# A two-block transformer kernel on one core: the mLSTM part re-cut around g3, ba0 and ba1, o/i/f as 260 + 260 columns, and six held blocks at the end

## The chip, the cores and the metric

The kernel runs on one core of one Trainium2 chip. The metric is the device time of one execution in microseconds, the median of three runs. The profile is that of one further execution.

## What is computed

Two blocks over 256 tokens of width 1024, batch 1. All in float32; a weight product is made as three products of rounded parts (high x high, high x low, low x high).

```
h = modulate(rms_norm(x, g_pre_mix), shift_m, scale_m)
q_a,k_a,v_a, q_m,k_m,v_m, o_m,i_m,f_m, g_a,g_m = split(h @ w_in)
y_a = sliding_window_attention(rope(q_a), rope(k_a), v_a, sinks)
q_m,k_m = split(silu(causal_depthwise_conv([q_m,k_m])))
h_m = mlstm_chunkwise(q_m, k_m, v_m, i_m + b_i, f_m + b_f)      # 4 heads of 128, chunks of 64
    # num = (q k' * w_intra) v + w_inter * q C_prev ; den likewise ; h = num / max(|den|, exp(-m))
y_m = sigmoid(o_m) * head_layer_norm(h_m, mlstm_norm_w)
merged = sigmoid(g_a) * (y_a @ w_branch_attn) + sigmoid(g_m) * (y_m @ w_branch_mlstm)
x = x + gate_m * rms_norm(merged @ w_out)
x = x + gate_f * rms_norm(swiglu(modulate(rms_norm(x))) @ w_ffn_down)
# second block: gMLP and RWKV-7 mixing, then the same kind of feed-forward, and at its very end
x = layer_norm(ALPHA * x + gt2 * f, ln2_g, ln2_b)
```

## The kernel before

Every engine's program is one list written out by hand; semaphores tie the lists together. The weights come as a stream of 512 KB blocks through six slots of `raw` (SyncE issues a block when VectorE has given up the slot, line 450). For each block ScalarE makes the rounded high part `whi` (`split`, line 559) and VectorE the low part `wlo` (`prepare`, line 416), in `HL = 4` slots each; ScalarE may write a slot when TensorE has done the block that was in it (`blocks_done`). Blocks named c0 to c21 belong to the modulation vectors: VectorE sums them into `acc` (lines 433 and 437), and TensorE adds them up over the partitions in `part(d)` with products of one column (line 1914).

The order of items on TensorE is o_if, qm, km, vm, g0, qa, kva, g1, g2, g3, ba0, ba1, bm0, bm1, wo0, wo1, then the feed-forward. `tokens_out` (lines 1958 to 1960) puts tokens on the rows of the result, `features_out` (1983 to 1985) features. The names that matter here:

- o_if has 520 columns: i and f (8) and o (512). The 8 go to banks 4 and 5, the 512 to the item's own pair. ScalarE takes the sigmoid of o into `osig` (line 610).
- `between(i)` runs on TensorE behind g3's blocks 0, 1, 2: states of the mLSTM (`chunk_kv`) and the turned attention scores (`turn_scores`, line 2141), which wait for ScalarE's exponentials (`score_exps`, 693 and 695).
- Behind g3: the attention's products with v for 128 tokens (o0, line 2165), `part(3)`, the same for the other 128 (o1, line 2172), `intra_part(0)` (line 2183: the mLSTM's product within its chunks for tokens 0 to 127), the turns of y_a (line 2204), `inter_part(0)` (2194: the part with the carried states), `intra_part(1)`, `inter_part(1)`.
- VectorE divides y_a by the sums of scores (1317), adds inter to intra (`take_inter`, 1328), makes the low half `yal` of the turned y_a (1352), takes each head's mean and variance (`head_stats`, 1341 to 1346), and multiplies by `osig` (1382) to `ym`. ScalarE copies intra out of its bank (722), copies `yah` (728), takes the root of the variances (734) and scales the eight heads (739).
- `turn_ym` (2217) turns ym on TensorE behind ba1; ScalarE copies `ymh`, VectorE makes `yml` (1388); bm0 and bm1 need both. `by_gate` (1375) multiplies a branch by its gate and frees its banks.
- `down_block(t, m, c)` (2245 to 2247) adds block t of the last weights for row half m and column half c into bank 4 + 2m + c. The first 22 - 4 blocks run block by block; the last four, held in the four slots, run row by row: (m, c) = (0,0), (0,1), (1,0), (1,1), each over all four blocks, so that a quarter of the result is done early. VectorE then weighs a quarter and adds it (`residual`, lines 1422, 1819, 1508) and finishes a row half in `last_rows` (1848 to 1853).

Of the kernel before, what the change touches and what calls it, by code (L numbers as in the profile page):

```python
# [8 lines left out]
D = 1024  # L9
P = 128  # L10
MT = S // P
# [9 lines left out]
HL = 4  # L21
# [126 lines left out]
def build(nc, A, out):  # L148
# [5 lines left out]
    with ctx:  # L154
# [24 lines left out]
        hl = rounded("hl", ARENA + 2048, [KT, S])  # L179
        raw = sb("raw", [P, RAW, SLOT])  # L180
# [206 lines left out]

        def part_place(d):
            return {0: (0, 0), 1: (1, 0), 2: (2, 0), 3: (4, 0), 4: (6, 0), 5: (4, 0), 6: (4, 6), 7: (4, 7),
                    8: (2, 8), 9: (2, 9), 10: (6, 0), 11: (4, 0)}[d]  # L390
# [16 lines left out]
        def prepare_on(eng, me, name, part=slice(None)):  # L407

            for b in sorted(at_block[name] + at_block.get(with_piece(name), []))[part]:
# [4 lines left out]
                if g is not None:  # L414
                    eng.wait_ge(sem("hi_ready"), g + 1)
                    eng.tensor_tensor(wlo[:, g % HL, 0:nk * width], raw[:, b % RAW, 0:nk * width],  # L416
                                      whi[:, g % HL, 0:nk * width].bitcast(fp), ALU.subtract)\
# [98 lines left out]
        def _(act):  # L516
# [34 lines left out]
            def split(name, part=slice(None)):  # L551

                for b in at_block[name][part]:
                    _, _, nk, width, _, count, g = order[b]
                    act.wait_ge(sem(f"raw{b % RAW}_in"), count)
                    if g >= HL:

                        act.wait_ge(sem("blocks_done"), g - HL + 1)
                    act.activation(whi[:, g % HL, 0:nk * width], raw[:, b % RAW, 0:nk * width], ACT.Copy)\  # L559
# [50 lines left out]
            act.activation(osig[:, 0, :], b0[:, :], ACT.Sigmoid).then_inc(sem("osig_ready"), 1)  # L610
            freed("o_if", act.activation(osig[:, 1, :], b1[:, :], ACT.Sigmoid))
# [97 lines left out]

            take_turned(0, 2)  # L710
            split("ba0", slice(0, 1))
            take_turned(2, 4)
            split("ba0", slice(1, 2))
# [5 lines left out]
            for m in range(MT):  # L719
                for h2 in range(2):  # L720
                    act.wait_ge(sem("intra_done"), 2 * m + h2 + 1)
                    act.activation(intra[:, m, 2 * h2:2 * h2 + 2, :],
                                   bank[4 + h2][:, 0:258].rearrange("p (h n) -> p h n", h=2),
                                   ACT.Copy).then_inc(sem("intra_ready"), 1)
                if m == 0:
                    for i in range(MT):
                        act.wait_ge(sem("ya_turned"), i + 1)
                        act.activation(yah[:, :, i * P:(i + 1) * P],
                                       bank[2 + i][:, :].rearrange("p (i n) -> p i n", i=4),
                                       ACT.Copy).then_inc(sem("yah_ready"), 1)  # L730

            split("bm0", slice(0, 1))
            act.wait_ge(sem("hvar_ready"), 1)
            act.activation(st[:, 112:120], st[:, 112:120], ACT.Sqrt).then_inc(sem("hstd_ready"), 1)
            act.wait_ge(sem("hvar_ready"), 2)
            for m in range(MT):
                for h in range(HM):
                    n = 4 * m + h
                    ins = act.activation(intra[:, m, h, 0:128], intra[:, m, h, 0:128], ACT.Identity,
                                         bias=st[:, 144 + n:145 + n], scale=st[:, 112 + n:113 + n])  # L740
                ins.then_inc(sem("hstd_ready"), 1)
            split("bm0", slice(1, 2))
# [239 lines left out]
        def _(dve):  # L982
# [137 lines left out]
            item("o_if")  # L1120
            dve.wait_ge(sem("spreads"), 3 * 16)
            for m in range(MT):
                TT(st[:, 240 + 8 * m:248 + 8 * m], bank[4 + m][:, 0:8], bsm[:, 0:8], ALU.add)\
                    .then_inc(sem("if_ready"), 1)

            dve.wait_ge(sem("osig_ready"), 1)
# [186 lines left out]
            collect_part(3)  # L1313
            prepare("ba1", slice(0, 1))
            for m in range(MT):
                dve.wait_ge(sem("o_done"), m + 1)
                TT(ya[:, m, :].rearrange("p (h c) -> p h c", h=HQ), bank[m][:, :].rearrange("p (h c) -> p h c", h=HQ),
                   bcast(st[:, 32 + 8 * m:40 + 8 * m], 64), ALU.mult)\
                    .then_inc(sem("ya_ready"), 1)
            prepare("ba1", slice(1, 2))  # L1320
# [1291 lines left out]
```

## Time and profile before

| | |
|---|---|
| median of 3 runs | 861.46 us (861.17 to 861.91) |
| the profiled execution | 863.23 us, its span 861.4 us |
| TensorE busy | 809.8 us, 94% |
| VectorE busy | 640.3 us, 74% |
| ScalarE busy | 390.0 us, 45% |
| mean granted clock of TensorE | 0.98 |

Busy times count instructions that run, not waits. Products on TensorE are pipelined: one of 512 columns is shown with about 0.39 us but the next starts 0.23 us later, so starts are to be compared and not durations.

### The profile page before, as it was taken

The numbers are of one execution on the slowest core, as the hardware profiler recorded it, in microseconds if no ns is written. First come the engines' busy times: TensorE is split into PE (matmuls) and PEld (weight loads), VectorE is DVE, ScalarE is ACT, GpSimd is POOL, SyncE is SP. The second block draws the span as 40 slices with busy tenths as digits, with TensorE's granted clock in tenths as the row PEclk, the third lists the DMA queues.
The fourth block names the chain that finished last, engine by engine and source line by source line (L and its number), as shares of the span: only waits on it lengthen the run. The fifth ranks groups of instructions, "written<-read, shape, count | busy, mean of one in ns | idle before, by whom it ended". The sixth has DMA issues, their size and how long they took to land.

```text
span 861.4 us, 16653 instructions
## 1 busy us (share of the span) xinstructions
PE 809.8 (94%) x7026; PEld 739.0 (86%) x7026; DVE 640.3 (74%) x841; ACT 390.0 (45%) x540; POOL 12.6 (1%) x32
## 2 busy tenths in 40 slices
PE   2899999899799999999998999989998999999995
PEld 2798998898678999999887987889977999999883
DVE  5859878858978877867877899887478777455447
ACT  3346843834255444444244884521134544444331
POOL 0100000000000000000001000000000000000000
PEclk9899999979999999999999999999999999999998
DMA  9974656761766978988883634610043669465521
GB/s 364 334 257 157 192 177 213 232 206 56 240 224 234 348 241 279 324 269 305 332 302 98 226 121 134 208 53 4 27 149 122 211 221 346 153 190 176 198 95 49
DMA packets 95832, 173.71 MB, mean 202 GB/s; under 512 B 7575, under 2 KB 55038, under 8 KB 95758
## 3 DMA queue, kind: packets, MB, share of 16 engines
q1 hardware_dynamic: 92784, 165.86, 57.5%
q0 software_dynamic: 1744, 5.84, 2.1%
q8 instruction: 55, 0.90, 0.4%
q10 hardware_dynamic: 1230, 0.95, 0.4%
q14 instruction: 19, 0.16, 0.1%
HBM read 171.58 MB, written 1.05 MB: 200 GB/s over the span
## 4 chain that ended last, share of the span: by engine, by line
PE 74%; DVE 17%; ACT 4%; issue 2%; DMA 2%; DVEq 0%; SPq 0%; ACTq 0%
PE bank L1983 13%; PE bank L1985 12%; PE bank L1984 12%; PE bank L2245 4%; PE bank L2247 4%; PE bank L2246 4%; DVE acc L437 3%; PE bank L2415 3%; PE bank L1958 2%; DVE wlo L416 2%; PE bank L1959 2%; PE bank L1960 2%; PE bank L1914 1%; DMA raw<-in_w_in 1%; DVE arena L437 1%
## 5 line engine op out<-in xcount | busy, mean ns | idle before, releaser
L559 ACT ACTIVATE whi<-raw 128x1024 fp32r<-128x1024 f32 (+2 forms) x218 | 226.8, 1051 | 271.3 <-PE bank L1985 122.6
L416 DVE TENSOR_TENSOR wlo<-raw,whi 128x1024 fp32r<-128x1024 f32 (+2 forms) x218 | 261.9, 1214 | 110.1 <-ACT whi L559 106.8
L1983 PE MATMUL bank<-hh,whi 128*128 128x256 f32 x1016 | 287.0, 282 | 3.2 <-DVE hl L1071 2.9
L1985 PE MATMUL bank<-hh,wlo 128*128 128x256 f32 x1016 | 285.2, 281 | 0.0
L1984 PE MATMUL bank<-hl,whi 128*128 128x256 f32 x1016 | 285.2, 281 | 0.0
L1983 PEld LDWEIGHTS bank<-hh,whi 128*128 128x128 f32 x1016 | 192.3, 189 | 6.1 <-issue 5.6
L1985 PEld LDWEIGHTS bank<-hh,wlo 128*128 128x128 f32 x1016 | 191.6, 189 | 0.0
L1984 PEld LDWEIGHTS bank<-hl,whi 128*128 128x128 f32 x1016 | 191.4, 188 | 0.1
L437 DVE SCALAR_TENSOR_TENSOR acc<-raw,cc,acc 128x1024 f32<-128x1024 f32 x77 | 98.6, 1280 | 7.3 <-DMA raw<-in_w_ada 3.4
L2245 PE MATMUL bank<-whi,ffh 128*128 128x512 f32 x176 | 69.6, 396 | 0.7 <-DVE wlo L416 0.7
L2246 PE MATMUL bank<-wlo,ffh 128*128 128x512 f32 x176 | 69.3, 394 | 0.0
L2247 PE MATMUL bank<-whi,ffl 128*128 128x512 f32 x176 | 69.2, 393 | 0.0
L1958 PE MATMUL bank<-whi,hh 128*128 128x512 f32 (+2 forms) x112 | 41.8, 373 | 0.7 <-DVE wlo L416 0.7
L1959 PE MATMUL bank<-wlo,hh 128*128 128x512 f32 (+2 forms) x112 | 41.3, 369 | 0.0
L1960 PE MATMUL bank<-whi,hl 128*128 128x512 f32 (+2 forms) x112 | 41.2, 368 | 0.0
L2245 PEld LDWEIGHTS bank<-whi,ffh 128*128 128x128 f32 x176 | 33.1, 188 | 9.1 <-DVE wlo L416 1.6
L2247 PEld LDWEIGHTS bank<-whi,ffl 128*128 128x128 f32 x176 | 33.1, 188 | 7.7
L2246 PEld LDWEIGHTS bank<-wlo,ffh 128*128 128x128 f32 x176 | 33.0, 188 | 7.4
L812 ACT ACTIVATE ffh<-arena 128x512 fp32r<-128x512 f32 x22 | 13.9, 632 | 46.8 <-DVEq L1480 46.8
L2415 PE MATMUL bank<-arena 64*64 64x64 f32 x896 | 28.0, 218 | 3.1 <-DVEq L1700 1.8
L2415 PEld LDWEIGHTS bank<-arena 64*64 64x64 f32 x896 | 27.1, 134 | 4.0 <-DVEq L1700 1.9
L1994 PE MATMUL bank<-cst 128*128 128x256 bf16 x220 | 28.7, 293 | 0.0
(430 smaller groups left out, 1027.4 us busy)
## 6 DMA issues: line engine op xcount, KB each, us to landing
raw<-in_w_ada SPq DMA_DIRECT2D x96, 512.0 KB, 5.0
raw<-in_w_in SPq DMA_DIRECT2D x54, 512.0 KB, 4.6
raw<-in_w_ffn_in SPq DMA_DIRECT2D x88, 256.0 KB, 3.7
raw<-in_w_ffn_gate SPq DMA_DIRECT2D x44, 256.0 KB, 4.0
raw<-in_w_ffn_up SPq DMA_DIRECT2D x44, 256.0 KB, 5.1
raw<-in_w_ffn_down SPq DMA_DIRECT2D x22, 512.0 KB, 5.5
raw<-in_w_ffn_out SPq DMA_DIRECT2D x22, 512.0 KB, 3.2
raw<-in_w_out SPq DMA_DIRECT2D x16, 512.0 KB, 5.1
```

The lines of the kernel that those rows point to most:

```text
L416: eng.tensor_tensor(wlo[:, g % HL, 0:nk * width], raw[:, b % RAW, 0:nk * width], whi[:, g % HL, 0:nk * width].bitcast(fp), ALU.subtract)\
L437: eng.scalar_tensor_tensor(to, x, by, to, ALU.mult, ALU.add)\
L559: act.activation(whi[:, g % HL, 0:nk * width], raw[:, b % RAW, 0:nk * width], ACT.Copy)\
L1958: mm(dsts[m], xh[:, kk_, t], wh[:, k, c], start=first, stop=False)
L1959: mm(dsts[m], xh[:, kk_, t], wl[:, k, c], start=False, stop=False)
L1983: mm(o, wh[:, k, c], xh[:, kk_, :], start=first, stop=False)
L1984: mm(o, wh[:, k, c], xl[:, kk_, :], start=False, stop=False)
L1985: last = mm(o, wl[:, k, c], xh[:, kk_, :], start=False, stop=end)
L2245: mm(o, ffh[:, t, x], wh[:, 0, cs], start=(t == 0), stop=False)
L2246: mm(o, ffh[:, t, x], wl[:, 0, cs], start=False, stop=False)
L2247: return mm(o, ffl[:, t, x], wh[:, 0, cs], start=False, stop=(t == FT - 1))
L2415: last = mm(bank[4 + 2 * (n % 2) + h][r, L * (q % 8):L * (q % 8) + L], lhsT[r, q, :], rhs[r, q, :], start=True, stop=True)
```

## The change

1. o_if is cut at column 260 instead of 8: columns 260 to 519 go to banks 4 and 5, columns 0 to 259 to the item's own pair. Each of 48 pairs of products (8 and 512 columns) becomes a pair of 260 and 260. ScalarE takes two sigmoids of 252 columns and two of 260. i and f are read from the end of banks 4 and 5.
2. `intra_part(0)` moves between g3's blocks, into banks 6 and 7; behind g3 stand o0, `inter_part(0)`, `part(3)`, o1, the first turn of y_a, `intra_part(1)`, the second turn, `inter_part(1)`.
3. VectorE and ScalarE normalise y_m by halves of 128 tokens: `head_stats(0)`, `head_var(0)` and `head_shift(0)` move ahead of ba0, and ScalarE's scaling of half 0 with them.
4. `turn_ym` moves from behind ba1 to behind its first block.
5. In the second feed-forward six blocks are held: the last two have places of their own, `whl` and `wll`, in the memory of `hh` and `hl`, free when gf10 is done. `last_rows(0)` moves ahead of `residual(1, 0)`.

```diff
+        whl = rounded("whl", ARENA, [2, D])
+        wll = rounded("wll", ARENA + 2048, [2, D])
...
+        HELD = HL + 2
+
+        def weight_place(g):
+            j = g - (split_n - 2)
+            return (whl[:, j], wll[:, j]) if j >= 0 else (whi[:, g % HL], wlo[:, g % HL])
...
-                    if g >= HL:
+                    if g >= split_n - 2:
+
+                        act.wait_ge(sem("blocks_done"), place[f"gf{FT // 2 - 1}"][2])
+                    elif g >= HL:
...
-            act.activation(osig[:, 0, :], b0[:, :], ACT.Sigmoid).then_inc(sem("osig_ready"), 1)
-            freed("o_if", act.activation(osig[:, 1, :], b1[:, :], ACT.Sigmoid))
+
+            for m in range(MT):
+                act.activation(osig[:, m, 260:512], bank[4 + m][:, 0:252], ACT.Sigmoid)
+            act.activation(osig[:, 0, 0:260], b0[:, 0:260], ACT.Sigmoid).then_inc(sem("osig_ready"), 1)
+            freed("o_if", act.activation(osig[:, 1, 0:260], b1[:, 0:260], ACT.Sigmoid))
...
             take_turned(2, 4)
+            take_intra(0, 6)
             split("ba0", slice(1, 2))
...
+            normalise(0)
+            for i in range(MT):
+                act.wait_ge(sem("ya_turned"), i + 1)
+                act.activation(yah[:, :, i * P:(i + 1) * P], bank[2 + i][:, :].rearrange("p (i n) -> p i n", i=4),
+                               ACT.Copy).then_inc(sem("yah_ready"), 1)
+                if i == 0:
+                    take_intra(1, 4)
+            split("bm0", slice(0, 1))
+            normalise(1)
             split("bm0", slice(1, 2))
...
             take_inter(0)
+            collect_part(3)
+            prepare("ba1", slice(0, 1))
+            divided(0)
+            head_stats(0)
+            head_var(0)
+            divided(1)
+            head_shift(0)
+            prepare("ba1", slice(1, 2))
+            gains(1, v1T[:, v1["g_pre_ffn"][0]:v1["g_pre_ffn"][1]])
...
             take_inter(1)
...
+            head_stats(1)
+            head_var(1)
+            weigh_y(0)
+            head_shift(1)
             prepare("bm0", slice(0, 1))
...
+            weigh_y(1)
             by_gate("ba0", 0)
...
-            tokens_out("o_if", 512, modulated, extra=512, half_ready=0)
+            tokens_out("o_if", 260, modulated, extra=260, half_ready=0)
...
+                if i == 1:
+
+                    pe.wait_ge(sem("state_ready"), 4)
+                    intra_part(0, 6)
+                    turn_scores(2, 4)
+                if i == 2:
+                    turn_scores(4, 6)
+                    pe.wait_ge(sem("intra_ready"), 2)
+                    chunk_kv(2, 6)
...
+            turn_ya(0)
+            pe.wait_ge(sem("piece_used"), 4)
+            intra_part(1, 4)
+            turn_ya(1)
             inter_part(1)
...
-            features_out("ba1", four, (yah, yal))
-            turn_ym()
+            features_out("ba1", four, (yah, yal), inside={0: turn_ym})
...
-                for t in range(FT - HL):
+                held = HELD if n else HL
+                for t in range(FT - held):
...
             ln_var(0)
+            dve.wait_ge(sem("ln_var"), 5)
+            last_rows(0)
             dve.wait_ge(sem("rows_done"), 9)
             residual(1, 0, bank[6])
-            dve.wait_ge(sem("ln_var"), 5)
-            last_rows(0)
```

TensorE's list from g3's last block to ba0, before:

```order
L1985 MATMUL bank<-hh,wlo 128x256
L2165 MATMUL bank<-arena 128x64 x8
L1914 MATMUL bank<-cst,acc 128x1 x8
L2172 MATMUL bank<-arena 128x64 x16
L2183 MATMUL bank<-arena,bc 128x129 x4
L2204 MATMUL bank<-cst,arena 128x128 x8
L2194 MATMUL bank<-arena 64x129 x8
L2183 MATMUL bank<-arena,bc 128x129 x4
L2194 MATMUL bank<-arena 64x129 x8
L1983 MATMUL bank<-yah,whi 128x256
```

The same place of the changed kernel (2224 and 2234 are o0 and o1, 1952 the piece, 2185 intra, 2196 inter, 2240 the turns of y_a):

```order
L2023 MATMUL bank<-hh,wlo 128x256
L2224 MATMUL bank<-arena 128x64 x8
L2196 MATMUL bank<-arena 64x129 x8
L1952 MATMUL bank<-cst,acc 128x1 x8
L2234 MATMUL bank<-arena 128x64 x16
L2240 MATMUL bank<-cst,arena 128x128 x4
L2185 MATMUL bank<-arena,bc 128x129 x4
L2240 MATMUL bank<-cst,arena 128x128 x4
L2196 MATMUL bank<-arena 64x129 x8
L2021 MATMUL bank<-yah,whi 128x256
```

One intra part has left this stretch, the first inter part stands ahead of the piece, and the two turns are parted by the other intra part.

VectorE's list behind the end of `head_stats(1)` up to yml, before (416 low halves of blocks, 1375 gate, 1382 weighing of y, 1388 yml):

```order
L1359 TENSOR_TENSOR st<-st 128x8
L1360 SCALAR_TENSOR_TENSOR st<-st 128x8
L1361 RECIPROCAL st<-st 128x8
L416 TENSOR_TENSOR wlo<-raw,whi 128x1024
L1365 SCALAR_TENSOR_TENSOR st<-st 128x8
L1375 TENSOR_TENSOR arena<-bank,arena 128x512 x2
L1382 TENSOR_TENSOR arena<-arena 128x512 x2
L1388 TENSOR_TENSOR yml<-bank,ymh 128x4x128 x2
```

The same place of the changed kernel (427 low halves, 1417 gate, 1385 weighing, 1425 yml):

```order
L1372 TENSOR_TENSOR st<-st 128x4
L1373 SCALAR_TENSOR_TENSOR st<-st 128x4
L1374 RECIPROCAL st<-st 128x4
L1385 TENSOR_TENSOR arena<-arena 128x512
L1379 SCALAR_TENSOR_TENSOR st<-st 128x4
L427 TENSOR_TENSOR wlo<-raw,whi 128x1024
L1385 TENSOR_TENSOR arena<-arena 128x512
L1417 TENSOR_TENSOR arena<-bank,arena 128x512 x2
L1425 TENSOR_TENSOR yml<-bank,ymh 128x4x128 x2
```

The variance is that of one half here; y's first half is weighed before the block of bm0 and its second before the gate of ba0.

## Rows read from the trace of the kernel before

**Rows 1.** The page: TensorE's busy time, and the chain that ended last by engine
```profile
PE 809.8 (94%) x7026; PEld 739.0 (86%) x7026; DVE 640.3 (74%) x841; ACT 390.0 (45%) x540; POOL 12.6 (1%) x32
PE 74%; DVE 17%; ACT 4%; issue 2%; DMA 2%; DVEq 0%; SPq 0%; ACTq 0%
```
**Rows 2.** Waits of TensorE: total us, times, longest us
```profile
PE bank L1958 <- DVE wlo L416: 5.6, 4, 3.8
```
**Rows 3.** Timeline, TensorE at o_if and qm's start: start, us, instruction, [idle before]
```profile
35.29 0.25 PE L1958 MATMUL bank<-whi,hh 128*128 128x8 f32 x1
...
36.63 0.48 PE L1958 MATMUL bank<-whi,hh 128*128 128x512 f32 x1
...
51.87 0.28 PE L1983 MATMUL bank<-hh,whi 128*128 128x256 f32 x1
51.99 0.27 PE L1984 MATMUL bank<-hl,whi 128*128 128x256 f32 x1
```
**Rows 4.** Timeline, TensorE from g3's second block to ba0
```profile
169.07 1.09 PE L2141 MATMUL bank<-cst,xn 128*128 128x128 f32 x8 [2.40 <-ACT st L695]
...
177.83 1.89 PE L2165 MATMUL bank<-arena 128*128 128x64 f32 x16
180.19 2.14 PE L1914 MATMUL bank<-cst,acc 128*128 128x1 f32 x16 [0.47 <-DVE acc L437]
182.20 7.07 PE L2172 MATMUL bank<-arena 128*128 128x64 f32 x32
189.06 2.04 PE L2183 MATMUL bank<-arena,bc 128*128 128x129 f32 x8
190.88 1.60 PE L2204 MATMUL bank<-cst,arena 128*128 128x128 f32 x8
192.42 1.11 PE L2194 MATMUL bank<-arena 128*64 128x129 f32 x16
193.46 1.16 PE L2183 MATMUL bank<-arena,bc 128*128 128x129 f32 x8
```
**Rows 5.** One window: length, busy per engine, granted clock, DMA share, GB/s
```profile
181.80:192.00 10.20, 10.20 (x50) 10.20 (x50) 4.06 (x7) 0.79 (x3) 0.00 (x0) 0.50 0.37 126
```
**Rows 6.** Timeline around ba0 and bm0, of VectorE, ScalarE and TensorE
```profile
195.63 1.38 DVE L1328 SCALAR_TENSOR_TENSOR arena<-bank,st,arena 128x129 f32<-128x129 f32 x4
...
203.23 1.23 DVE L416 TENSOR_TENSOR wlo<-raw,whi 128x1024 fp32r<-128x1024 f32 x1
...
209.28 1.33 DVE L1388 TENSOR_TENSOR yml<-bank,ymh 128x512 fp32r<-128x512 f32 x2 [0.73 <-ACT ymh L745]
...
204.62 3.19 ACT L739 ACTIVATE arena<-arena,st 128x128 f32<-128x128 f32 x8 [1.24 <-DVEq L1366]
...
210.66 0.39 PE L1983 MATMUL bank<-ymh,whi 128*128 128x256 f32 x1 [1.41 <-DVE yml L1388]
...
226.15 0.75 PE L1958 MATMUL bank<-whi,mgh 128*128 128x512 f32 x1 [3.84 <-DVE wlo L416]
```
**Rows 7.** Timeline of the end: ScalarE, TensorE, VectorE
```profile
834.13 1.06 ACT L559 ACTIVATE whi<-raw 128x1024 fp32r<-128x1024 f32 x1 [1.73 <-PE bank L2247]
...
842.04 0.50 PE L2245 MATMUL bank<-whi,ffh 128*128 128x512 f32 x1 [0.35 <-DVE wlo L416]
...
848.62 0.69 DVE L1422 TENSOR_TENSOR xn<-bank,gg 128x512 f32<-128x512 f32 x1 [0.32 <-PE bank L2247]
...
853.65 0.68 DVE L1422 TENSOR_TENSOR xn<-bank,gg 128x512 f32<-128x512 f32 x1
```
**Rows 8.** Timeline, VectorE and ScalarE, low and high parts of blocks, 37 to 47 us
```profile
37.22 3.54 DVE L416 TENSOR_TENSOR wlo<-raw,whi 128x1040 fp32r<-128x1040 f32 x3
46.34 2.36 DVE L416 TENSOR_TENSOR wlo<-raw,whi 128x1024 fp32r<-128x1024 f32 x2 [5.58 <-ACT whi L559]
...
45.25 2.01 ACT L559 ACTIVATE whi<-raw 128x1024 fp32r<-128x1024 f32 x2 [6.89 <-issue]
```
**Rows 9.** Timeline, VectorE: start of the convolution, and of the mLSTM columns
```profile
66.70 0.41 DVE L1144 TENSOR_SCALAR arena<-arena,v1T 128x256 f32<-128x256 f32 x1 [0.88 <-ACT arena L620]
...
111.46 0.19 DVE L1221 COPY st<-bank 128x32 f32<-128x32 f32 x1 [3.28 <-PE bank L2048]
```

More of the change, by code:

```diff
@@ L708, in take_turned, with take_intra @@
                                    ACT.Copy).then_inc(sem("pT_ready"), 1)
+            def take_intra(m, at):
+                for h2 in range(2):
+                    act.wait_ge(sem("intra_done"), 2 * m + h2 + 1)
+                    act.activation(intra[:, m, 2 * h2:2 * h2 + 2, :],
+                                   bank[at + h2][:, 0:258].rearrange("p (h n) -> p h n", h=2),
+                                   ACT.Copy).then_inc(sem("intra_ready"), 1)
             take_turned(0, 2)
@@ L717, in _, with normalise @@
             split("ba1", slice(1, 2))
[L719 to L736, printed above, removed]
+            def normalise(m):
+                q = slice(112 + 4 * m, 116 + 4 * m)
+                act.wait_ge(sem("hvar_ready"), 2 * m + 1)
+                act.activation(st[:, q], st[:, q], ACT.Sqrt).then_inc(sem("hstd_ready"), 1)
+                act.wait_ge(sem("hvar_ready"), 2 * m + 2)
                 for h in range(HM):
@@ L1312, in _ @@
                 step(dve.reciprocal(st[:, 32 + 8 * m:40 + 8 * m], st[:, 32 + 8 * m:40 + 8 * m]))
[L1313 to L1320, printed above, removed]
-            gains(1, v1T[:, v1["g_pre_ffn"][0]:v1["g_pre_ffn"][1]])
             def take_inter(m):
@@ L1887, in weights @@
                 pe.wait_ge(sem(f"{who}_blocks"), count)
[L1888 removed]
+                hi, lo = (w[:, 0:nk * width].rearrange("p (k n) -> p k n", k=nk) for w in weight_place(g))
+                return i, nk, hi, lo
             def part(d):
@@ L2196, in inter_part, with between, turn_ya @@
                     last.then_inc(sem("inter_done"), 1)
-            intra_part(0)
-            for m in range(MT):
+            def between(i):
+                if i == 0:
+                    pe.wait_ge(sem("sw_ready"), 2)
+                    chunk_kv(1, 6)
+                    turn_scores(0, 2)
+                if i == 1:
[6 more added lines that the diff above has]
+                    chunk_kv(2, 6)
+            pe.wait_ge(sem("piece_used"), 3)
+            features_out("g3", four, modulated, inside={i: (lambda i=i: between(i)) for i in range(3)})
+            pe.wait_ge(sem("pT_ready"), 6)
+            pe.wait_ge(sem("va_ready"), 1)
+            for h in range(HQ):
+                g = h // 4
+                last = mm(bank[0][:, 64 * h:64 * h + 64], pT[:, h, :], va[:, 0, 64 * g:64 * g + 64],
+                          start=True, stop=True)
+            last.then_inc(sem("o_done"), 1)
+            pe.wait_ge(sem("state_ready"), 6)
+            inter_part(0)
+            part(3)
+            for h in range(HQ):
+                g = h // 4
+                for kb in range(2):
+                    last = mm(bank[1][:, 64 * h:64 * h + 64], pT[:, 8 + 2 * h + kb, :], va[:, kb, 64 * g:64 * g + 64],
+                              start=(kb == 0), stop=(kb == 1))
+            last.then_inc(sem("o_done"), 1)
+            def turn_ya(m):
                 pe.wait_ge(sem("ya_ready"), m + 1)
-                if m == 0:
-                    pe.wait_ge(sem(f"pair{place['g3'][0] % 2}_free"), place["g3"][0] // 2 + 1)
                 for i in range(4):
@@ L2260, in feed_forward @@
                     for c in range(2):
-                        for t in range(FT - HL, FT):
+                        for t in range(FT - held, FT):
                             last = down_block(t, m, c)
```

90 lines of the change are left out of this document (32 added, 58 removed).

## The prediction

> **What bounds the kernel now.** I read the page first: the shares of busy time and the chain that ended last. TensorE is busy for 94% of the span and carries 74% of the chain, VectorE 17% [rows 1]. So a change can gain in three ways only: fewer cycles on TensorE, filled gaps on TensorE, or a shorter end after its last product. The view of waits says that the gaps are few: the longest waits for VectorE are 5.6 us in four pieces, at the start of wo0 [rows 2]. I then read the timeline of each engine at the four places that the diff touches. Every time below is on the scale of the profile before; an event that comes earlier only because everything before it is earlier keeps its number.
>
> At o_if (35.29 to 51.87 us) TensorE has no gap [rows 3]. Each of its four blocks has 12 products of 8 columns and 12 of 512. The first 12 take 36.63 - 35.29 = 1.34 us, 0.112 us from start to start, though they move 8 columns; the whole block takes 16.58 / 4 = 4.15 us, so the wide ones have 2.81 / 12 = 0.234 us. In the item behind it the step between products of 256 columns is 51.99 - 51.87 = 0.12 us. Small products are nearly as dear as products of 256 columns.
>
> Between g3's end and ba0 (177.83 to 195.8 us) TensorE is nominally busy, but from 181.8 to 192 us at half clock, 0.50 granted, the level of 1.2 GHz [rows 4, 5]. Ahead of the fall stand a gap of 0.47 us and 16 products of one column. The second 129-wide intra part takes 1.16 us at full clock, the first 2.04 at half. There is also a gap of 2.40 us before the turn of scores at 169.07, ended by ScalarE's exponentials.
>
> After ba1, TensorE turns ym and waits for yml: bm0 starts at 210.66 us [rows 6]. VectorE then does a chain of fixed work (ba1's and bm0's gates, four pieces, the low half of merged, wo0's first block) and wo0 starts at 226.15, after an idle stretch of 3.84 us. From bm0's start on, this stretch is VectorE's.
>
> At the end TensorE's last but one row block goes to VectorE at 848.62, but `last_rows(0)` stands ahead of the last residual, which starts at 853.65 [rows 7].
>
> **The parts, worked out.**
>
> *o, i, f as 260 + 260.* Removed: 48 products of 8 columns and 48 of 512, 16.58 us [rows 3]. Added: 96 of 260 columns. No row has 260; the bounds are 0.112 us (8 columns) and 0.234 us (512), the nearest row 0.12 us (256). With 0.12: 96 x 0.12 = 11.5 us, 5.0 us less. Not all of it arrives. Block 1's low half is made at 37.22 + 1.2 = 38.4, and block 0 now ends at 35.29 + 2.88 = 38.17: 0.3 us of waiting. Three more blocks end at 47.1. ScalarE's queue splits qm's first block only at 45.25, behind its own issues of small transfers (its 6.89 us of idleness are put down to issue), and VectorE's part starts at 46.34 and takes some 1.2 us [rows 8]. So qm starts at 47.6 and not at 51.87: **4.3 us** earlier. ScalarE's two sigmoids become four of half the width; it waits for TensorE there, and the splits for km have until 59 us, so I cost them at nothing (without that cover about 0.6 us).
>
> Does it stay? VectorE starts the convolution 0.88 us after its last work, when ScalarE has copied qm, and later waits 3.28 us for TensorE's columns at 111.46 [rows 9]. Both starts hang on TensorE's progress, so they move with it, and all that is released by them too. The transfers from 52 us on are issued when VectorE gives up a slot of `raw`, so they move as well. I keep 4.3.
>
> The Trainium skill, "TensorE: Matmul & The Clock Gate", section on 56 against 53.3 ns, gives start to start at full clock as the columns by 2.4 GHz plus about 2.5 ns. By that rule an 8-column product would cost 5.8 ns and o_if the same before and after, so this part would bring nothing and the sum would be 857.1. The trace disagrees for narrow products: 112 ns.
>
> *The first intra part between g3's blocks.* It goes into the 2.40 us gap before the turn at 169.07, where its four heads (1.16 us at full clock) are free: states and banks are there by 166 us. ScalarE takes it over behind `take_turned(2, 4)`, some 0.8 us, which delays ba0's second split and with it VectorE by some 0.35 us. Behind g3 the order is now o0, inter 0, piece 3, o1, turn, intra 1, turn, inter 1. At full clock inter 0 adds 1.1 us and covers the gap of 0.47. Piece 3's one-column products remain, so I expect the clock to fall as before, near the end of piece 3, and o1 to take its 7 us again: o1 ends at 180.8 + 2.05 + 7.0 = 189.85 (189.06 before). What follows is shorter by one intra part (2.04) and inter 0 (1.1): first turn to 190.75, intra 1 to 192.6, second turn to 193.2. But ba0 needs yal, and the halves of y now compete with it. VectorE must have `divided(1)` done (190.7) before the shift, ScalarE then scales four heads (half of its 3.19 us for eight [rows 6]) to 192.6, copies yah 0, takes intra 1 (0.8), copies yah 1 to 194.5; yal follows at 195.2. So ba0 starts at 195.2, not 195.8: **0.6 us**. If the clock stays up, this same chain on ScalarE and VectorE holds ba0 at about 194.5.
>
> *y by halves, ym's turn inside ba1.* From ba0's start: its two blocks take 5.7 us (as every pair of 24 x 0.12), to 200.9; ba1's first block to 203.8. Inter 1 of VectorE takes 1.3 us; statistics and variance of both halves took from 196.9 to 203.2, so one half takes about 3.5, to 200.1. Half 0 of y is weighed by 200.8; ScalarE scales half 1 from 201.1 to 202.7; its weighing ends at 203.4. The turn in ba1 at 203.8 thus has 0.4 us to spare. It takes about 1.0 us, ba1 ends at 207.65, and yml is ready at 206.4 (before 210.6), 1.2 us to spare. bm0 starts at 207.65 instead of 210.66: **3.0 us**, the 0.6 among them. The VectorE chain from bm0's end to wo0 is the same instructions, so wo0 moves by 3.0 too, to 223.1, with the same idle stretch before it. Behind it VectorE feeds wo0 block by block; all shifts.
>
> *Six held blocks, last rows reordered.* The row-wise part now has 6 x 3 products of 0.2315 us, 4.17 us for a quarter where it had 2.78. It starts 5.56 us earlier, at 833.85. ScalarE may split block 19 at 834.13 as before [rows 7]; 20 and 21 follow at some 1 us each (two take 2.01), VectorE at 1.14 to 1.18 us each (three take 3.54) [rows 8], so block 21 is ready at 838.7, and TensorE, which wants it at 837.3, waits some 1.2 us in all, against 0.35 now. TensorE ends 0.9 us later. VectorE, however, has residual (0,1) at 844, `last_rows(0)` to 849.3 and residual (1,0) to 851.4, and is free when the last quarter arrives at 851.97 + 0.33 = 852.3, not 853.65: **1.35 us** gained. Without the waits it would be 2.2.
>
> **Sum.** 4.3 + 3.0 + 1.35 = 8.65 us. The profiled execution: 863.23 us, span 861.4; it becomes 854.6 and 852.8. It stands 1.8 us over the median; from the median 861.46 the forecast is **852.8 us**.
>
> **Rivals.**
> - *The clock falls elsewhere* (0.14). Half clock comes in stretches, and every one falls at another instruction once the work moves. If the one before bm0 or a later one is missed, TensorE gains 1.5 to 3 us where it is the bound: 850.5. Speaks for it: the cost of a stretch on real work is half its length. Against: behind g3 and at wo0 other engines hold the time.
> - *The second half waits for VectorE after all* (0.13). The turn in ba1 has 0.4 us to spare; if ym or yml is later than reckoned by some 3 us, the 3.0 go: 855.8.
> - *o_if's time is given back* (0.12), to a transfer or split late between 52 and 158 us: 857.1. Speaks for it: VectorE is nearly full there; against: its starts hang on TensorE.
> - *No change to speak of* (0.05): both of these, 860.
> - *Slower* (0.05): 260 columns fall out of the fast path. The other parts give 4.35; the total turns into more than 0.2% (1.7 us) slower when a product of 260 costs over (16.58 + 6.05) / 96 = 0.236 us, just above the row of 512. At plain-float price (four products of 129 in 1.16 us, so 0.58 for 260) it would be 861.46 - 4.35 + 55.7 - 16.6 = 896. Against it: 256 columns at 0.12.
>
> **How the numbers follow.** Likeliest (0.51): all parts as worked out, 851.3 to 854.4 (the stalls of the end and the clock behind g3 either way). The range takes in the clock's case from 849.7 and reaches to 857.3, the case of o_if lost; outside are slower, no change and the edges of the others, 0.17. A measurement of this kernel tells about 0.2%, 1.7 us. Faster 0.90, same 0.05, slower 0.05.
>
> **What the profile after would show.** Right: o_if's 96 products in about 12 us, qm waiting briefly for VectorE; the gap at 166.7 partly filled; no wait of bm0 for yml; 1 to 1.5 us of waits for low halves in the held blocks, and no VectorE work between the last quarter and its residual. Wrong: a step over 0.13 us at 260 columns; ScalarE's normalising ending after ba1's first block; a new long wait between 52 and 158 us; a slow stretch over dense products that was not there.

## The result, and the profile after

The changed kernel takes 852.16 us (median of 4 executions, 851.24 to 852.72), the kernel before beside it 861.64 us (4, 861.17 to 861.91). The ratio is 0.989, with a 95% interval of 0.9875 to 0.9905. A second set of executions of the same two kernels gave 851.81 against 860.70 us, ratio 0.9895 (0.9877 to 0.9912). The forecast was 852.8 us, faster.

The profiled execution took 851.24 us, its span is 849.4 us. Below stand TensorE's and VectorE's busy time and the chain by engine from the page of the changed kernel, which answer to [rows 1], then those of TensorE's waits that the change bears on. The two longest of all, 9.4 us for a transfer and 5.3 us for ScalarE, were there before (9.2 and 5.2) and nothing in the change touches them.

```profile
PE 805.3 (95%) x7026; PEld 736.3 (87%) x7026; DVE 641.1 (75%) x845; ACT 389.7 (46%) x543; POOL 12.6 (1%) x32
PE 76%; DVE 16%; ACT 3%; issue 2%; DMA 2%; DVEq 0%; SPq 0%; ACTq 0%
```
```profile
PE bank L1996 <- DVE wlo L427: 5.7, 3, 3.8
...
PE bank L2284 <- DVE wlo L427: 0.8, 2, 0.4
PE bank L2179 <- ACT st L712: 0.8, 1, 0.8
...
PE bank L2284 <- DVE wll L427: 0.3, 2, 0.2
```

No wait of bm0 for yml is left (1.41 us in [rows 6]), and the turn of scores waits 0.8 us where it waited 2.40 [rows 4].

TensorE at o_if and at qm's start, from the timeline of the changed kernel (start, us, instruction, idle before), beside [rows 3]:

```profile
34.56 0.35 PE L1996 MATMUL bank<-whi,hh 128*128 128x260 f32 x1 [0.39 <-DVE hl L1094]
...
38.80 0.39 PE L1996 MATMUL bank<-whi,hh 128*128 128x260 f32 x1 [1.14 <-DVE wlo L427]
...
47.50 0.30 PE L2021 MATMUL bank<-hh,whi 128*128 128x256 f32 x1
```

From 38.80 to 47.50 us run three blocks of 24 products: 8.70 / 72 = 0.121 us each, from start to start. Block 1 had to wait 1.14 us for its low half, and qm for nothing.

TensorE behind g3, beside [rows 4], and three windows over it (length, busy by engine, granted clock, DMA share, GB/s), beside [rows 5]:

```profile
162.24 1.05 PE L2185 MATMUL bank<-arena,bc 128*128 128x129 f32 x8
164.05 1.09 PE L2179 MATMUL bank<-cst,xn 128*128 128x128 f32 x8 [0.76 <-ACT st L712]
...
172.81 1.89 PE L2224 MATMUL bank<-arena 128*128 128x64 f32 x16
174.64 1.11 PE L2196 MATMUL bank<-arena 128*64 128x129 f32 x16
175.67 1.95 PE L1952 MATMUL bank<-cst,acc 128*128 128x1 f32 x16
177.48 6.49 PE L2234 MATMUL bank<-arena 128*128 128x64 f32 x32
183.77 1.06 PE L2240 MATMUL bank<-cst,arena 128*128 128x128 f32 x4
184.62 1.93 PE L2185 MATMUL bank<-arena,bc 128*128 128x129 f32 x8
```
```profile
177.50:178.20 0.70, 0.70 (x8) 0.70 (x8) 0.51 (x2) 0.68 (x2) 0.00 (x0) 0.94 0.92 360
178.20:188.40 10.20, 10.20 (x54) 9.87 (x55) 7.56 (x23) 4.15 (x10) 0.00 (x0) 0.50 0.37 114
188.40:190.00 1.60, 1.60 (x19) 1.43 (x16) 1.53 (x5) 0.00 (x0) 0.00 (x0) 1.00 0.43 177
```

The intra part stands ahead of the turn of scores, and the gap of 0.47 us behind o0 is gone. The clock falls all the same, for as long as before.

The end, from the timelines of TensorE and VectorE, beside [rows 7]:

```profile
825.73 0.50 PE L2284 MATMUL bank<-whi,ffh 128*128 128x512 f32 x1 [0.39 <-DVE wlo L427]
826.87 0.50 PE L2284 MATMUL bank<-whl,ffh 128*128 128x512 f32 x1 [0.17 <-DVE wll L427]
828.00 0.50 PE L2284 MATMUL bank<-whl,ffh 128*128 128x512 f32 x1 [0.17 <-DVE wll L427]
```
```profile
835.69 1.28 DVE L1885 SCALAR_TENSOR_TENSOR xt<-xt,st,bc 128x1024 f32<-128x1024 f32 x1
...
838.54 0.68 DVE L1459 TENSOR_TENSOR xn<-bank,gg 128x512 f32<-128x512 f32 x1
...
841.63 0.69 DVE L1459 TENSOR_TENSOR xn<-bank,gg 128x512 f32<-128x512 f32 x1 [0.95 <-PE bank L2286]
```

`last_rows(0)` is done before residual (1,0) now, and the last residual waits for TensorE.

**Where the time went.** The table takes the start of the same instruction in each trace and shows how much shorter each stretch is than in the profiled execution of before (us; minus is longer). The last line is the sum, the difference of the spans.

| stretch | changed | again | e1 | e2 | e3 | e4 | e5 | e7 | e8 | e10 | e11 |
|---|---|---|---|---|---|---|---|---|---|---|---|
| start to o_if | 0.73 | -1.38 | -1.72 | 0.02 | -1.66 | 0.25 | -0.92 | 1.21 | 0.21 | 0.07 | 0.46 |
| o_if to qm | 3.64 | 5.01 | 3.96 | 0.01 | 0.01 | 4.49 | 4.94 | 4.99 | 2.45 | 4.64 | 3.94 |
| qm to o0 | 0.65 | 0.09 | 0.56 | 0.75 | 0.13 | 0.11 | 0.75 | 0.04 | 0.50 | -0.24 | -1.34 |
| o0 to ba0 | 1.91 | 1.90 | -0.18 | 0.04 | 2.88 | 2.36 | 2.59 | 1.90 | -0.17 | 1.92 | 2.71 |
| ba0 to bm0 | 2.53 | 2.54 | -0.01 | -0.01 | 2.52 | 2.54 | 0.80 | 2.52 | 0.00 | 2.54 | 2.54 |
| bm0 to wo0 | 0.11 | 0.12 | 0.03 | 0.02 | 0.12 | 0.11 | 0.02 | 0.11 | 0.02 | 0.21 | 0.11 |
| wo0 to 729 us | 1.21 | 1.19 | 0.01 | 1.60 | -1.87 | -0.31 | 1.25 | 1.22 | 1.57 | 1.22 | 1.20 |
| the end | 1.22 | 1.25 | 0.00 | 1.23 | -0.26 | 2.77 | 1.23 | 2.77 | 0.02 | 1.22 | 2.76 |
| sum | 12.00 | 10.72 | 2.65 | 3.66 | 1.87 | 12.32 | 10.66 | 14.76 | 4.60 | 11.58 | 12.38 |

Three lines are not the change's: the stretch to o_if, that from qm to o0 (but for the intra part in it) and that behind wo0 differ, and the last by up to 3.5 us, also between kernels whose code there is that of before (e2 for all three). These are differences between executions. The first of them goes with the granted clock ahead of o_if: it was 1.00 from 30 us on in the changed kernel and in e7, which began o_if at 34.56 and 34.08 us; it was 0.50 from 32 to 35 us in before, which began it at 35.29; and it was 0.50 from 29 or 30 us on until 36 us or later in again, e1, e3 and e5, which began it at 36.2 to 37.0. The two windows below, which begin at the same instruction, show the third: before first, then the changed kernel.

```profile
526.50:530.00 3.50, 3.50 (x9) 2.76 (x10) 3.43 (x3) 0.59 (x1) 0.00 (x0) 0.51 0.27 99
```
```profile
516.90:520.30 3.40, 3.40 (x15) 2.78 (x16) 3.33 (x3) 0.93 (x2) 0.00 (x0) 1.00 0.29 103
```

In the profiled execution of before TensorE ran here at 0.51, in that of the changed kernel at 1.00, and the lead grows by 1.6 us there (from 9.57 at 491 us to 11.13 at 547; by 572 us it is 10.78). So the profiles differ by 12.0 us and the medians by 9.5.

### The profile page after: what moved, and what is told of

Its sections match the earlier page's. It is cut to its first block, busy times and chain, and to the rows that moved or that the text cites. A ratio compares the mean times of both kernels' runs of the same rounds, so it can differ in the third digit from the quotient of the medians.

```text
span 849.4 us, 16656 instructions
## 1 busy us (share of the span) xinstructions
PE 805.3 (95%) x7026; PEld 736.3 (87%) x7026; DVE 641.1 (75%) x845; ACT 389.7 (46%) x543; POOL 12.6 (1%) x32
## 4 chain that ended last, share of the span: by engine, by line
PE 76%; DVE 16%; ACT 3%; issue 2%; DMA 2%; DVEq 0%; SPq 0%; ACTq 0%
PE bank L2021 14%; PE bank L2023 13%; PE bank L2022 13%; PE bank L2284 4%; PE bank L2286 4%; PE bank L2285 4%; PE bank L2455 3%; DVE acc L448 3%; DVE wlo L427 2%; PE bank L1996 2%; PE bank L1998 2%; PE bank L1997 2%; PE bank L1952 1%; DMA raw<-in_w_in 1%; DVE arena L448 1%
## 5 line engine op out<-in xcount | busy, mean ns | idle before, releaser
L427 DVE TENSOR_TENSOR wlo<-raw,whi 128x1024 fp32r<-128x1024 f32 (+2 forms) x216 | 259.0, 1214 | 99.8 <-ACT whi L573 96.1
L2284 PE MATMUL bank<-whi,ffh 128*128 128x512 f32 x168 | 66.5, 396 | 0.8 <-DVE wlo L427 0.8
L2285 PE MATMUL bank<-wlo,ffh 128*128 128x512 f32 x168 | 66.1, 393 | 0.0
L2286 PE MATMUL bank<-whi,ffl 128*128 128x512 f32 x168 | 66.1, 393 | 0.0
L1996 PE MATMUL bank<-whi,hh 128*128 128x512 f32 (+2 forms) x112 | 40.0, 357 | 2.3 <-DVE wlo L427 1.9
L1998 PE MATMUL bank<-whi,hl 128*128 128x512 f32 (+2 forms) x112 | 39.4, 352 | 0.0
L1997 PE MATMUL bank<-wlo,hh 128*128 128x512 f32 (+2 forms) x112 | 39.3, 351 | 0.0
```

Source lines behind the costliest of these rows:

```text
L427: eng.tensor_tensor(lo[:, 0:nk * width], raw[:, b % RAW, 0:nk * width], hi[:, 0:nk * width].bitcast(fp), ALU.subtract)\
L1996: mm(dsts[m], xh[:, kk_, t], wh[:, k, c], start=first, stop=False)
L1998: last = mm(dsts[m], xl[:, kk_, t], wh[:, k, c], start=False, stop=end)
L2284: mm(o, ffh[:, t, x], wh[:, 0, cs], start=(t == 0), stop=False)
L2285: mm(o, ffh[:, t, x], wl[:, 0, cs], start=False, stop=False)
L2286: return mm(o, ffl[:, t, x], wh[:, 0, cs], start=False, stop=(t == FT - 1))
```

## The experiments

### One part at a time: e1_oif, e3_ba, e2_tail

Each is the kernel before with one part of the diff, in full: the cut of o_if at 260 (e1); everything between g3 and bm0 (e3); the six held blocks with `last_rows(0)` moved (e2).

```diff
-            tokens_out("o_if", 512, modulated, extra=512, half_ready=0)
+            tokens_out("o_if", 260, modulated, extra=260, half_ready=0)
```

> The kernel before with the cut of o_if at 260 alone. Theory (the steps of the prediction): o_if's 96 products step by 0.12 us, qm starts about 4.3 us earlier and all behind it keeps that: 857.3 us, ratio 0.995; in the trace the first scores of g1's end, the piece behind g2 and the first state product behind g3's first block all stand 4.3 us earlier, and so does bm0. Rival 1 (the time is given back by a late transfer or split): the lead shrinks between 52 and 158 us, ratio 0.997 to 1. Rival 2 (the clock): the lead stays, but a slow stretch falls elsewhere or is missed and the ratio is off by up to 0.002 to 0.003 either way.

> The kernel after with o_if as 8 + 512 and the end as before: only the first intra part, y by halves and the turn inside ba1. Theory as on record: ba0 0.6 us and bm0 3.0 us earlier, 858.5 us, ratio 0.9965. The trace of the kernel after showed more, 5.3 us from g3 to wo0; if that is the order of work and not the clock, this kernel gives 856.3, ratio 0.994. Rival (the clock and one transfer had a good day in that execution): the trace here shows 3.0 to 3.5 us and the ratio is 0.996.

> The kernel before with six held blocks and the last rows reordered, nothing else. Theory: TensorE waits some 1.2 us in the held blocks and ends 0.9 us later, the last residual starts 1.35 us earlier: 860.2 us, ratio 0.9984. Rival (the waits eat it): ratio 1.0. The two are told apart by the trace, where the time from the first held product to the end of the span was 861.4 - 839.4 = 22.0 us with four held; with six it must be 22.0 + 5.56 - 1.35 = 26.2 or 27.6.

Measured against 862.32 us for before (21 executions): e1 857.42 us, ratio 0.9939 (0.9918 to 0.9959); e3 856.44, ratio 0.9938 (0.9915 to 0.9962); e2 860.46, ratio 0.9974 (0.9956 to 0.9992). For e1 857.3 us had been expected and for e2 860.2. Each part gains by itself. The three ratios multiply to 0.985, the whole is 0.989; with intervals of 0.2% on each, that neither shows nor excludes a loss in common. The traces add up better: outside the three lines named above, each column of the table has its gain in the rows of its own part, and 0.3 us at most, either way, in those of the others. In e1 o_if's gain of 3.96 us is not given back between qm and 729 us. It would have been about 1 us more, but the first ten products of its o_if ran at half clock, 0.216 us from start to start, as the first of these two windows shows:

```profile
37.00:39.10 2.10, 2.10 (x11) 2.10 (x10) 2.10 (x3) 2.10 (x3) 0.56 (x2) 0.50 0.73 210
39.30:49.60 10.30, 10.30 (x88) 10.30 (x87) 5.83 (x6) 3.08 (x3) 1.37 (x3) 1.00 0.95 288
```

For e3 two times were expected, 858.5 us by the forecast's steps and 856.3 us by what the trace of the changed kernel had shown; 856.44 is the second. In e3 the stretch from o0 to wo0 is 5.52 us shorter than before, where the changed kernel has 4.55. The difference is in o1:

```profile
184.00:188.40 4.40, 4.40 (x35) 4.40 (x34) 3.87 (x13) 1.13 (x1) 0.00 (x0) 0.81 0.71 243
```

Here o1, from 184.0 to 188.4 us in e3, had a granted clock of 0.81 and took 4.4 us; in the changed kernel it took 183.77 - 177.48 = 6.3 us at 0.56. The program of this stretch is the same in both, so it alone does not fix where the fall comes.

### The held blocks and the order at the end: e6_reorder, e9_held, e4_slots

e6 is before with the reorder alone, e9 before with the six held blocks alone. e4 is the changed kernel with the places given out differently: the third and fourth held blocks get `whl` and `wll`, and the last two get ordinary slots whose products are already done.

```diff
-            j = g - (split_n - 2)
-            return (whl[:, j], wll[:, j]) if j >= 0 else (whi[:, g % HL], wlo[:, g % HL])
+            j = g - (split_n - 4)
+            if j in (0, 1):
+                return whl[:, j], wll[:, j]
+            at = (g - 2 if j >= 2 else g) % HL
+            return whi[:, at], wlo[:, at]
```

> The kernel before with one edit: last_rows(0) ahead of the last residual's first part residual(1, 0). My theory: alone it brings next to nothing, since without more held blocks the last quarter reaches VectorE in the same moment and VectorE still has to do the same chain of work from about 845.9 to 853.5; at most 0.3 us of the end. The rival: the reorder is what gives the 1.25 us of the end, because it takes last_rows(0) from between the last quarter and its residual; then the time from part 11's products (729.1) to the end shrinks by 1.0 us or more.

> The kernel before with the six held blocks alone; last_rows(0) stays behind residual(1, 0). My theory: the two edits need each other. Held alone, VectorE gets three quarters of the result earlier but still has last_rows(0) (5.3 us) between residual(1, 0) and the last residual, so the last residual starts near 853.2 on its own scale and the end gains 0.3 to 0.6 us. The rival: six held blocks alone give the whole 1.25 us, and the order of last_rows is of no matter.

> The kernel after, but the two places outside the four slots go to the third and fourth of the six held blocks (free since gf10), and the last two take the slots that come free first. So their parts are ready before TensorE wants them. Theory: the waits for low parts in the held blocks (0.6 to 1.2 us) vanish and the end comes that much earlier: 851.3 us, ratio 0.988. Rival (VectorE's last rows bound the end): nothing changes, 852.2, since the residual of the last quarter waits for VectorE and not for TensorE.

From 729 us to the end e6 is 0.26 us shorter than before and e9 0.45, both as expected; both edits together (e2) give 1.23. The two small gains are of the size by which the same code differs there: e3, which has the end of before, is 0.26 us longer, e1 and e8 differ by 0.02 at most. The 1.23 us are well beyond that. VectorE's timeline of e9 shows why it takes both:

```profile
845.27 0.69 DVE L1435 TENSOR_TENSOR xn<-bank,gg 128x512 f32<-128x512 f32 x1 [1.72 <-PE bank L2261]
...
847.45 1.28 DVE L1861 SCALAR_TENSOR_TENSOR xt<-xt,st,bc 128x1024 f32<-128x1024 f32 x1
...
850.30 0.69 DVE L1435 TENSOR_TENSOR xn<-bank,gg 128x512 f32<-128x512 f32 x1
```

VectorE idles 1.72 us for residual (1,0) and then does the 2.85 us of `last_rows(0)` while the last quarter is ready (TensorE's last product starts at 849.03). e6 and e9 ran once each, at 859.63 and 859.89 us against 861.84: 2 us less, though their code differs only at the end and gains 0.3 and 0.5 us there. That is the size of what single executions differ by.

e4: 850.23 us, ratio 0.9847 (0.9823 to 0.9872), and the end 2.77 us shorter. The expected 0.6 to 1.2 us over the changed kernel were 1.55. Its timeline of TensorE has no idle time in the held blocks, and the last residual on VectorE is:

```profile
841.32 0.69 DVE L1463 TENSOR_TENSOR xn<-bank,gg 128x512 f32<-128x512 f32 x1 [0.94 <-PE bank L2290]
```

So the rule on when ScalarE may split a held block cost 1.5 us. In the changed kernel the first product of each of three blocks begins late, and the second, which uses the low half, later still. The steps from start to start are 0.78, 0.57 and 0.56 us at the first product and 0.34 at the second where 0.235 is usual, 1.5 us in all, though the view of waits shows 0.73.

### The turn inside ba1: e5_ym_out

The changed kernel with `turn_ym` behind ba1 again.

```diff
-            features_out("ba1", four, (yah, yal), inside={0: turn_ym})
+            features_out("ba1", four, (yah, yal))
+            turn_ym()
```

> The kernel after with the turn of ym behind ba1 as before. Theory: the turn starts 2.9 us later, ScalarE's copies and VectorE's low half follow it, and bm0 and wo0 start 1.8 us later than in the kernel after: ratio 0.990. Rival (VectorE holds bm0 anyway, the halves are what counts): no more than 0.3 us later, ratio 0.988.

Measured 852.23 us, ratio 0.9905 (0.9887 to 0.9923). By the times alone it can't be told from the changed kernel. By the trace ba0 to bm0 is 0.80 us shorter than before and not 2.53, and bm0 waits again, as TensorE's timeline of e5 shows:

```profile
199.89 1.04 PE L2257 MATMUL bank<-cst,arena 128*128 128x128 f32 x8
202.50 0.39 PE L2021 MATMUL bank<-ymh,whi 128*128 128x256 f32 x1 [1.57 <-DVE yml L1425]
```

Of the 2.53 us, 1.7 are the turn's place, as expected. The 0.8 us that are left belong to the rest of the change in this stretch, the halves of y; no run takes those away by themselves.

### The first intra part, and the piece: e10_intra, e11_piece

e10 is the changed kernel with `intra_part(0)` behind o0 again. e11 is e4 with the piece behind o1.

```diff
-                    intra_part(0, 6)
...
+            intra_part(0, 4)
```
```diff
-            part(3)
...
+            part(3)
```

> The changed kernel with one part undone: the first intra part goes back behind o0, into bank 4, and ScalarE takes it over before the gates instead of between g3's blocks. My theory: ba0's 1.9 us come from TensorE's shorter stretch between o0 and ba0, part of it the intra part that lay in the gap before the turn of scores; moved back it costs TensorE 1.1 us (full clock) to 2.0 us (half clock), so ba0 comes 1 to 2 us later than in the changed kernel and the lead at ba0 falls from 6.9 to about 5 to 6. The rival: ba0 is held by the chain of VectorE and ScalarE (divided, scaling of four heads, yah, yal) and not by TensorE; then ba0 moves by less than 0.4 us.

> The changed kernel with slots as in e4_slots and the piece with its 16 one-column products moved from before o1 to behind it (VectorE collects it behind head_shift(0)). It asks what stands ahead of the fall to half clock behind g3. My theory: the granted clock falls because TensorE does little in the gap and the one-column products ahead of o1; with the piece moved, o0, the inter part and o1 follow each other closely, o1 runs at full clock in about 3.8 us (6.5 before), and any half-clock stretch comes later, on the piece or the turns. ba0 then moves by no more than 1 us, since the chain of VectorE and ScalarE to yal holds it. The rival: the fall does not hang on the piece (products of 64 columns are enough for it), o1 still takes 6 us or more with the clock at 0.50, and ba0 stays within 0.3 us or comes later.

e10: 851.65 us, one execution. The stretch from o0 to ba0 is 1.92 us shorter than before, as in the changed kernel (1.91): against that kernel, with which the expectation compares it, ba0 did not move, so the rival came true and the theory of 1 to 2 us missed. But the clock was low for 6.8 us in e10 and for 10.2 in the changed kernel. e4, with 6.8 us too, has 2.36. Beside e4, then, the intra part behind o0 costs 1.04 us of TensorE and makes ba0 0.44 us later. TensorE ends o1 at 183.50 and VectorE ends half 0's variance only at 184.44, so VectorE was last there. In the changed kernel VectorE waited 1.07 us for o1 instead. One execution of each doesn't settle more.

e11: 850.85 us, one execution. Windows over o0 with inter (first), over o1 (second) and behind it (third):

```profile
174.70:177.60 2.90, 2.90 (x34) 2.69 (x33) 2.72 (x5) 1.85 (x2) 0.00 (x0) 1.00 0.95 320
177.60:181.40 3.80, 3.80 (x36) 3.77 (x34) 3.61 (x10) 3.77 (x5) 0.00 (x0) 1.00 0.93 318
181.40:190.00 8.60, 7.41 (x50) 6.50 (x48) 6.42 (x21) 3.63 (x10) 0.00 (x0) 0.60 0.38 125
```

o1 ran at full clock, in 3.6 us, and the fall came over the piece and the turns. ba0 came 2.71 us earlier than before, 0.35 more than in e4: the 2 to 3 us that o1 is shorter do not reach ba0. Here too VectorE's variance ends last (184.37, o1 181.25), and the moved piece adds a wait of 1.19 us of its own. It agrees with the theory that the one-column products precede the fall, but a single execution is no proof, since e3 had a late fall without moving them. What brings the fall stays open.

### How narrow a product may be: e8_128

Before with o_if cut as 392 + 128, one execution.

```diff
-            tokens_out("o_if", 512, modulated, extra=512, half_ready=0)
+            tokens_out("o_if", 392, modulated, extra=128, half_ready=0)
```

> The kernel before with o, i, f as 392 + 128 columns. Theory: a product has a floor of 0.112 us and above some 245 columns costs 0.45 ns a column, so 128 costs 0.112 and 392 some 0.18: o_if takes 48 x 0.292 = 14.0 us, between 16.6 and 11.6. Rival (the time is by columns alone, and 8 was dear for another reason, such as the bank it writes): 128 columns step by 0.06 us and o_if takes 11.5 us.

Start to start in e8, on TensorE's timeline:

```profile
35.32 0.27 PE L1960 MATMUL bank<-wlo,hh 128*128 128x128 f32 x1
...
36.55 0.39 PE L1959 MATMUL bank<-whi,hh 128*128 128x392 f32 x1
36.78 0.34 PE L1960 MATMUL bank<-wlo,hh 128*128 128x392 f32 x1
...
38.57 0.34 PE L1961 MATMUL bank<-whi,hl 128*128 128x392 f32 x1
```

128 columns: (36.55 - 35.32) / 11 = 0.112 us; 392: (38.57 - 36.78) / 10 = 0.179. The 96 products take 49.21 - 35.08 = 14.13 us (expected 14.0), and the stretch o_if to qm is 2.45 us shorter. 8 and 128 columns cost the same, 260 only 0.009 us more, so the rival (time by columns alone) fell: a narrow product has a floor, and the gain of an even cut comes from the products that stood on it.

### Again, and a better version: a2_after, e7_best

a2 is the changed kernel once more, the column "again" of the table. e7 is e4 with an edit that is to take o_if's waits away: block 1's low half is made between the two halves of h's scaling, and qm's first blocks are split before ScalarE issues its small transfers.

```diff
-            scale_h(0, second_half)
-            prepare("o_if", slice(1, 2))
+            scale_h(0, second_half, first_half=lambda: prepare("o_if", slice(1, 2)))
...
+            split("qm", slice(0, 2))
...
-            split("qm")
+            split("qm", slice(2, 4))
```

> The changed kernel once more, to stand beside the others on one chip and to show what of its trace repeats. Theory: the lead over the kernel before is 4.3 us at the state product behind g3's first block, 9 to 9.6 at wo0 and 1.2 at the end, whatever the clock does; ratio 0.988. Rival (a good day): the part between g3 and bm0 gains 3 us here and not 4.5.

> The places of the held blocks as in e4_slots, and at o_if VectorE makes the low half of block 1 between the halves of h, while ScalarE splits qm's first two blocks before it issues its small transfers. Theory: TensorE's wait of 1.14 us inside o_if goes, and o_if's end is followed by qm at once: 1.1 to 1.4 us better than e4_slots, ratio 0.983. Rival (block 1 is not what it waits for, h is; or qm's third block is then late behind the transfers): a new wait of the same size in o_if or at qm's third block, ratio 0.9847 as e4_slots.

a2 repeats what was asked of it: from o0 to bm0 it is 4.44 us shorter than before, as the changed kernel is, where the rival had 3, and the end 1.25. Its lead at wo0 is 8.28 us and not 9 to 9.6, since it began o_if 1.38 us later than before.

e7: 848.22 us against 860.70, ratio 0.9862 (0.9838 to 0.9885), the lowest median of all. The expected ratio, 0.983, was missed. e4 has 0.9847 beside its own executions of before, and the intervals overlap, so the times do not show that e7 is faster than e4. In the traces o_if to qm is 0.50 us shorter than in e4, and not 1.1 to 1.4: e4's o_if took 12.09 us in that execution, so little was left to gain. e7's o_if takes 45.67 - 34.08 = 11.59 us without a wait, 0.121 us a product, though it began earlier than any other; a2's took 11.57 us without the edit, but began at 36.67.

```profile
34.08 0.36 PE L2000 MATMUL bank<-whi,hh 128*128 128x260 f32 x1 [0.39 <-DVE hl L1099]
45.67 0.28 PE L2025 MATMUL bank<-hh,whi 128*128 128x256 f32 x1
```

## Why the prediction was right, point by point

**o, i, f as 260 + 260: right.** Forecast 4.3 us from o_if's start as it was, 0.12 us a product. Measured 0.121 us, and a lead of 4.37 us at qm and 4.28 at 138 us. That 4.37 is so near is in part chance. The parts of the sum differed: o_if began 0.73 us earlier, which is not the change's, and block 1 then waited 1.14 us and not 0.3, since its low half comes when ScalarE and VectorE have it, not when TensorE asks. From o_if to qm the gain is 3.64 us here and 3.94 to 5.01 in the other kernels with this cut. With an execution that starts later (again, 5.01 us) the wait is not there. The forecast wait before qm did not come: VectorE began the low half at 46.14 us, and qm's first product, at 47.50, was not held.

The rule of the Trainium skill that the prediction weighed ("TensorE: Matmul & The Clock Gate", section on 56 against 53.3 ns: columns by 2.4 GHz plus about 2.5 ns) would have had o_if the same before and after. The same section of the Trainium skill also says that a step never drops below about 25 ns, which the prediction left out when it put 5.8 ns for 8 columns; with it the even cut would bring 0.9 us (an estimate from that page: 48 x (25 + 216) ns against 96 x 111 ns). No run here agrees with either figure: 8 and 128 columns take 112 ns, and at 260, 392 and 512 columns the rows have 121, 179 and 232 ns, where by that rule they would have 111, 166 and 216.

**It stays: right.** The rival that gives o_if's time back (0.12) fell with e1: nothing is lost from 52 us to 729.

**ba0: the mis-sized term.** Forecast 0.6 us, measured 1.91 (and 1.90 to 2.88 in the other kernels with this part). The step was "I expect the clock to fall as before, near the end of piece 3, and o1 to take its 7 us again: o1 ends at ... 189.85". On before's scale (plus 5.02) o1 ended at 188.79. The half clock began at 178.2 + 5.02 = 183.2 and not at 181.8, so the piece and the start of o1 were at full clock, and o1 took 6.3 us. The chain behind it was reckoned at 4.5 us from `divided(1)` to ba0 and took 188.84 - 184.70 = 4.14. That is 1.06 and 0.36 us. "If the clock stays up, this same chain holds ba0 at about 194.5" had the right engines and a bound too high: in e3, with the clock mostly up, ba0 came 15.06 us behind o0, at 192.9. That the chain holds ba0 shows in e4, where the clock was back at 1.00 from 185.6 us on and TensorE waited for `yal`:

```profile
188.56 0.39 PE L2025 MATMUL bank<-yah,whi 128*128 128x256 f32 x1 [1.07 <-DVE yal L1405]
```

In the changed kernel yal was ready at 188.76 us and ba0 began at 188.84, right behind the last inter part, so there both ended together.

**bm0: right.** Forecast 2.4 us beyond ba0's, measured 2.53. The rival in which the second half waits for VectorE (0.13) did not come, and the spare times held: y was weighed 0.57 us before the turn (forecast 0.4), yml was ready 1.15 us before bm0 (forecast 1.2). wo0 kept its idle stretch:

```profile
216.58 0.77 PE L1996 MATMUL bank<-whi,mgh 128*128 128x512 f32 x1 [3.84 <-DVE wlo L427]
```

**The end: right in size.** Forecast 1.35 us, measured 1.22. TensorE ended 0.95 us later against its lead at 729 us (forecast 0.9); the waits shown are 0.73 us (forecast 1.2), and the slow second products make up the rest. "VectorE is free when the last quarter arrives" holds: it idles 0.95 us. "Without the waits it would be 2.2" was too low: e4 has 2.77, because it is also free of the 0.6 us that before lost at its own wait (842.04 us).

**The sum.** Forecast 8.65 us by parts; measured in the trace 4.28 + 1.91 + 2.53 + 0.11 + 1.22 = 10.05, and of the 1.4 us between them ba0 is 1.3. The profiled execution has 1.95 us more: 0.74 in the stretch before o0, which e2 has too with before's code there, and 1.2 behind wo0. The medians differ by 9.5 and, in the second set, 8.9 us. The forecast started from 861.46 and so ended at 852.8, 0.6 us from the median. So near a hit is partly luck: the parts came out 1.4 us larger than forecast in the traces, ba0 above all, and the medians show 0.6 to 1.2 us less than the traces' parts add up to, for which no run gives the reason. The prediction's reading of [rows 2], 5.6 us of waits "at the start of wo0", was too much as well: 3.8 of them are there. Nothing in the sum hangs on it.

**The clock as a rival** (0.14, 850.5 us) is in every trace to some degree. Where TensorE is the bound a stretch at half clock of 3.4 us costs about half its length (1.6 us at 526 us in before; in e11 the clock was at 0.51 from 107.5 to 114.5 us, twice as long as in the changed kernel, and its lead fell by 1.6 us there), and such stretches come or stay away from execution to execution, in code that is the same. Over the 21 executions of before the fastest (860.14 us) had a mean granted clock of 0.985 and the slowest (867.5 us) 0.976. How much of the clock is in the difference of the medians, no run separates.

## What to carry to other kernels

Where one part of a product's columns would be narrow, cut them evenly: here 8 and 128 columns took the same 0.112 us. The line through 260 (0.121 us) and 392 columns (0.179) reaches 0.112 us at about 240, an estimate of where the floor ends; no width between 128 and 256 was run. The gain stays if what follows waits for TensorE. When work is held back to shorten a tail, look at when the buffer of each held block comes free and at who serves it next; here the choice of the slot was worth as much as holding the blocks. Compare traces over the stretch that was changed, and not by their spans: stretches whose code is the same differed by 1 to 3 us between executions.

## What the runs showed of the hardware that was not expected

- A product with a weight load of its own takes 0.112 us at 8 columns and at 128, 0.121 at 260, 0.179 at 392 and 0.232 at 512 (the forecast's 0.2315).
- The product behind one that waited starts late too: 0.34 us from start to start where 0.235 is usual, three times at the end of the changed kernel and once in before (842.04 us). The view of waits shows only half of what such a stop costs, 0.73 of 1.5 us. Waiting need not be the cause: in before the step is 0.32 us (36.63 to 36.95 us) with no wait, where the width goes from 8 to 512 columns.
- The fall to half clock behind g3 came at different instructions and lasted 10.2, 6.8 or 3.4 us in executions whose program is the same there (changed kernel, e4, e3). At half clock (0.50 granted, 1.2 GHz) a product of 260 columns took 0.216 us in e1 where it takes 0.121 at 1.00.
- A load of ScalarE's table takes 1.28 us. It was done while the instruction that needs it still waited for another engine, so it cost nothing here. ScalarE's timeline of the changed kernel:

```profile
177.69 1.28 ACT L748 ACT_TABLE_LOAD   x1
183.03 0.21 ACT L748 ACTIVATE st<-st 128x4 f32<-128x4 f32 x1 [4.06 <-DVEq L1375]
```
